# A streaming encoder layer on eight cores: the head's loads and statistics in another order

## The reference, cut to what matters

```python
h = rmsnorm(x, g_pre)
xa, ba, ca, za, xb, zb, ga, gb = split(h @ w_in)     # 8 x 1024 columns
ya = ((ba * conv3(ca * xa)) * silu(za)) @ w_a_out
d_g = mean_W(xb_g) - xb_g                            # W in (2, 4, 8, 16) by channel group
yb = (((d_g @ w_grp[g]) * pool_scale) * silu(zb)) @ w_b_out
o = (sigmoid(ga) * ya + sigmoid(gb) * yb) @ w_o
x1 = x + rmsnorm(o, g_post)
out = x1 + (p @ w_ple) * sigmoid(x1 @ w_pgate)
```

## Time and profile before

| | |
|---|---|
| median of 3 timed runs | 755.54 us (755.41 to 755.64) |
| the profiled execution | 757.77 us |
| its span, slowest core | 756.1 us (core 0) |
| other cores | 749.6 to 753.0 us |
| TensorE busy | 735.2 us, 97% of the span |
| VectorE, GpSimd, ScalarE busy | 58%, 52%, 32% |
| DMA, mean over the span | 111 GB/s |

### The profile page before, as it was taken

One profiled execution on the slowest core, in us unless ns is written; L12 is line 12 of the kernel. 1 busy time (PEld: TensorE's weight loads), 2 busy tenths in 40 slices (PEclk: granted clock), 3 DMA queues, 4 the chain that ended last, 5 costly groups with the idle time before them and its releaser, 6 DMA issues.

```text
span 756.1 us, 13493 instructions; the slowest of 8 cores (749.6 to 756.1 us)
## 1 busy us (share of the span) xinstructions
PE 735.2 (97%) x4131; PEld 367.1 (49%) x4201; DVE 441.8 (58%) x745; ACT 245.6 (32%) x454; POOL 395.6 (52%) x498
## 2 busy tenths in 40 slices
PE   6899989999999999999999999999999999999997
PEld 3774434444444444454545454545554554554443
DVE  3567455575775656346464555567767456454755
ACT  3433333323221212243333433323332222214442
POOL 3332435548876873533435262637686856731552
PEclk9999999999999999999999999999999999999999
DMA  8989877756656856885364644335333606334564
GB/s 192 215 149 181 85 166 141 132 82 112 113 89 98 130 91 127 116 137 120 72 102 125 93 95 104 76 79 85 52 67 70 112 9 104 59 116 89 156 157 141
DMA packets 67034, 83.92 MB, mean 111 GB/s; under 512 B 35858, under 2 KB 37394, under 8 KB 66964
## 3 DMA queue, kind: packets, MB, share of 16 engines
q0 software_dynamic: 31152, 48.31, 42.2%
q1 hardware_dynamic: 35664, 34.66, 18.1%
q10 hardware_dynamic: 148, 0.08, 0.1%
HBM read 115.25 MB, written 9.26 MB: 165 GB/s over the span
## 4 chain that ended last, share of the span: by engine, by line
PE 91%; DMA 5%; DVE 1%; issue 1%; POOL 1%; ACT 0%; SPq 0%; DVEq 0%; ACTq 0%; POOLq 0%
PE ps L525 57%; PE ps L710 12%; PE ps L782 8%; PE ps L817 8%; DMA slab<-w_in 3%; PE ps L539 2%; PE ps L640 2%; PE ps L811 2%; DMA xt<-xp 2%; DVE qT L613 0%; POOL tmp L609 0%; POOL slab L412 0%; DVE tmp L719 0%; PE ps L487 0%; DVE qT L647 0%
## 5 line engine op out<-in xcount | busy, mean ns | idle before, releaser
L525 PE MATMUL ps<-hT,slab 128*128 128x512 bf16 (+1 forms) x1920 | 348.0, 337 | 1.7
L525 PEld LDWEIGHTS ps<-hT,slab 128*128 128x128 bf16 x1952 | 170.5, 98 | 171.9 <-issue 2.4
L412 POOL DMA_DIRECT2D slab<-w_in x128 | 70.8, 557 | 53.0 <-PE ps L525 37.8
L609 POOL TENSOR_TENSOR tmp<-XB 128x526 f32<-128x526 f32 (+1 forms) x40 | 41.6, 1041 | 74.9 <-ACT XB L595 74.0
L609 POOL TENSOR_TENSOR tmp<-tmp 128x524 f32<-128x524 f32 (+5 forms) x60 | 63.2, 1053 | 3.2 <-POOL tmp L609 0.4
L782 PE MATMUL ps<-wo_sb,mT 128*128 128x512 bf16 x268 | 61.8, 379 | 0.2
L525 PE MATMUL ps<-vT,slab 128*128 128x512 bf16 (+1 forms) x314 | 61.4, 346 | 0.3
L525 PE MATMUL ps<-qT,slab 128*128 128x512 bf16 (+1 forms) x313 | 61.1, 346 | 0.4
L613 DVE SCALAR_TENSOR_TENSOR qT<-tmp,XB 128x512 bf16<-128x512 f32 (+1 forms) x40 | 29.8, 744 | 43.8 <-POOL tmp L609 43.5
L583 ACT ACTIVATE tmp<-U,smallT 128x512 f32<-128x512 f32 (+1 forms) x40 | 30.0, 749 | 67.8 <-DVE U L580 56.4
L828 POOL TENSOR_TENSOR xt<-xt,tmp 128x512 f32<-128x512 f32 x24 | 32.2, 1343 | 36.9 <-DVE tmp L825 35.9
(11 more groups left out here) (108 smaller groups left out, 947.9 us busy)
## 6 DMA issues: line engine op xcount, KB each, us to landing
slab<-w_in POOLq DMA_DIRECT2D x128, 256.0 KB, 6.5
xt<-xp SPq DMA_DIRECT2D x30, 512.0 KB, 7.2
yp<-xt SPq DMA_DIRECT2D x14, 512.0 KB, 3.0
slab<-w_a_out POOLq DMA_DIRECT2D x16, 256.0 KB, 6.4
slab<-w_b_out POOLq DMA_DIRECT2D x16, 256.0 KB, 5.3
wo_sb<-w_o POOLq DMA_DIRECT2D x4, 512.0 KB, 7.5
hT<-w_pgate POOLq DMA_DIRECT2D x4, 512.0 KB, 8.5
xt<-xs SPq DMA_DIRECT2D x2, 512.0 KB, 4.3
```

Of the source, the lines that this page charges most:

```text
L412: OP('pool', lambda e, d: d(e.dma_start(out=v.ap[:], in_=src)), writes=[v], sem=dsem(v, "ld"), dur=0.56, mb=0.52, key=key, nb=nb, lat=2.5 ...
L525: ins = e.matmul(b.ap[:, 0:N], lhsT=w.ap[:, kk, :], rhs=act[:, kk, k.rel:k.rel + N], start=(kk == 0), stop=(kk == nk - 1))
L609: d(e.tensor_tensor(out=twin(o.ap, k, nlo, E), in0=a, in1=b_, op=ALU.add))
```

## The change

Six edits, all but one in the first 40 us.

1. The add of tile 0's statistic is placed ahead of the second g copy on VectorE (key of that copy from -5 to 5). The planned times of the g matmuls are changed, and the second set of warm matmuls has one matmul in place of three.
2. The first slab (xa, j = 0) is loaded as fp32 by SP, second in its queue, into `U`; ScalarE casts it to its slab buffer. The other five are still loaded by GpSimd.
3. Tiles 4 to 7 are loaded into the home of `w_o` (four halves of 4 KB per partition), which is free from the start. The loads of `w_o` wait for the last use of those tiles.
4. The first part of `smallT` (for j = 0 and 1) is issued by SP in place of ScalarE, with a later key (9 for 1).
5. The planned latency after L613 is 3.0 for 1.5, in all of phase 1. No instruction is added by it; it changes only the planned order.
6. `load_res` takes ops to wait for.

```diff
@@ -309,6 +309,8 @@
         p_x = mkpool("xt", 4, [128, D], F32)
         x_late = [Buf("xtU", U[:, 0:D]), Buf("xtXB", XB[:, 0:D])]
         p_x.free += x_late
+        p_xh = Pool("xh", [Buf(f"xh{i}", wo_sb[:, 2 * i:2 * i + 2, :].rearrange("p a c -> p (a c)").bitcast(F32)) for i in range(4)])
+        xh_ops = []
         p_t = mkpool("tmp", 9, [128, TBW], F32)
         p_h = mkpool("hb", 3, [128, D], BF16)
         p_xT = mkpool("x1T", 2, [128, 8, 128], BF16)
@@ -373,8 +375,8 @@
         for h in range(2):
             OP('act', lambda e, d, h=h: d(e.dma_start(out=grow[h].ap[0:1, 0:512], in_=g_pre[0:1, h * 512:(h + 1) * 512])),
                writes=[grow[h]], sem=dsem(grow[h], "ldg"), dur=0.4, mb=0.002, key=-20 + h)
-        for j0, j1, key in ((0, 2, 1.0), (2, 8, 22.0)):
-            OP('act' if j0 == 0 else 'sp', lambda e, d, j0=j0, j1=j1: d(e.dma_start(out=smallT[:, j0:j1, :], in_=small.rearrange("p (j c) -> p j c", j=8)[:, j0:j1, :])),
+        for j0, j1, key in ((0, 2, 9.0), (2, 8, 22.0)):
+            OP('sp', lambda e, d, j0=j0, j1=j1: d(e.dma_start(out=smallT[:, j0:j1, :], in_=small.rearrange("p (j c) -> p j c", j=8)[:, j0:j1, :])),
                writes=[res(f"smallT{j}") for j in range(j0, j1)], sem=fsem(f"ld_small{j0}"), dur=0.4, mb=0.04 * (j1 - j0), key=key, nb=key)
         jb = val(p_b)
 
@@ -387,18 +389,18 @@
         gh = [val(p_b) for h in range(2)]
         for h in range(2):
             OP('pe', lambda e, d, h=h: d(e.matmul(gh[h].ap[:, :], lhsT=one.ap[0:1, 0:128], rhs=grow[h].ap[0:1, 0:512], start=True, stop=True)),
-               reads=[one, grow[h]], writes=[gh[h]], dur=1.7 - 0.6 * h, key=-8 + h)
+               reads=[one, grow[h]], writes=[gh[h]], dur=2.06, key=-8 + h)
             OP('dve', lambda e, d, h=h: d(e.tensor_copy(out=g_bc[:, h * 512:(h + 1) * 512], in_=gh[h].ap[:, :])),
-               reads=[gh[h]], writes=[res(f"g_bc{h}")], dur=0.69, key=-5)
-        OP('pe', lambda e, d: f_warm(e, d, 3), reads=[zb], writes=[jb], dur=0.7, key=-6)
+               reads=[gh[h]], writes=[res(f"g_bc{h}")], dur=0.69, key=-5 if h == 0 else 5)
+        OP('pe', lambda e, d: f_warm(e, d, 1), reads=[zb], writes=[jb], dur=0.43, key=-6)
 
         def load_gpost(key):
             OP('sp', lambda e, d: d(e.dma_start(out=g_bc[:], in_=g_post[0:1, :].partition_broadcast(128))),
                writes=[res("g_bc0"), res("g_bc1")], sem=fsem("ld_g"), dur=0.4, mb=0.5, key=key, nb=key)
 
-        def load_res(name, dst, src, k0, k1, key, extra=()):
+        def load_res(name, dst, src, k0, k1, key, extra=(), after=()):
             OP('pool', lambda e, d: d(e.dma_start(out=dst[:, k0:k1, 0:D], in_=src[k0 * 128:k1 * 128, :].rearrange("(k p) c -> p k c", p=128))),
-               writes=[res(f"{name}{k}") for k in range(k0, k1)] + list(extra), sem=fsem(f"ld_{name}{k0}"), dur=0.6 + 0.2 * (k1 - k0), mb=0.52 * (k1 - k0), key=key, nb=key)
+               writes=[res(f"{name}{k}") for k in range(k0, k1)] + list(extra), sem=fsem(f"ld_{name}{k0}"), dur=0.6 + 0.2 * (k1 - k0), mb=0.52 * (k1 - k0), key=key, nb=key, after=after)
 
         def load_wgrp(key):
             OP('pool', lambda e, d: d(e.dma_start(out=wgrp_sb[:], in_=w_grp.rearrange("(g k p) c -> p g k c", g=4, k=2, p=128))),
@@ -454,11 +456,23 @@
             return stats[:, row, gi:gi + 1]
 
 
+        slab0 = []
+
+        def first_slab():
+            v = val(p_w)
+            uu = [res("U0"), res("U1")]
+            OP('sp', lambda e, d: d(e.dma_start(out=U[:, 16:16 + D], in_=w_in[S_XA * 1024:S_XA * 1024 + 128, :])), writes=uu, sem=fsem("ld_first"), dur=0.4, mb=0.52, key=-25.5)
+            OP('act', lambda e, d: d(e.copy(out=v.ap[:].rearrange("p k c -> p (k c)"), in_=U[:, 16:16 + D])), reads=uu, writes=[v], dur=1.05, key=3.9)
+            slab0.append(v)
+
         def phase0(tl, key, by_pe):
             gi = tl.gi
-            x = val(p_x)
+            early = by_pe and gi >= 4
+            x = val(p_xh if early else p_x)
             kx = key - (30 if by_pe else 8)
             OP('sp', lambda e, d: d(e.dma_start(out=x.ap[:], in_=tl.x)), writes=[x], sem=dsem(x, "ld"), dur=0.4, mb=0.52, key=kx, nb=kx)
+            if by_pe and gi == 0:
+                first_slab()
             h = val(p_h)
             ss, rs = res(f"ss{gi}"), res(f"rs{gi}")
             OP('act', lambda e, d: d(e.activation(out=h.ap[:], in_=x.ap[:], func=AF.Square, scale=1.0 / 32.0, accum_out=stat(0, gi))),
@@ -493,6 +507,8 @@
                        reads=[b] + (first if n else []), writes=first if len(parts) > 1 and n == 0 else [ht], dur=0.69 if gi else 0.6, key=key)
                 else:
                     OP('sp', lambda e, d, hv=hv: d(e.dma_start_transpose(out=dst, in_=hv.ap[:])), reads=[hv], writes=[ht], sem=dsem(hv, "tr"), dur=1.3, mb=0.7, key=key)
+            if early:
+                xh_ops.extend(x.ops)
 
         def blkview(ap, k):
             if k.samp:
@@ -611,7 +627,7 @@
                 cur, lo, w = o, nlo, w * 2
             qr = res(f"qT{j}_{k.idx}")
             OP('dve', lambda e, d, cur=cur: d(e.scalar_tensor_tensor(out=actview(qT, j, k), in0=twin(cur.ap, k, 16, E), scalar=1.0 / W, in1=uwin(XB, k, 16, E), op0=ALU.mult, op1=ALU.subtract)),
-               reads=[cur, xr], writes=[qr], dur=d_t, key=key + 7 * dk, lat=1.5)
+               reads=[cur, xr], writes=[qr], dur=d_t, key=key + 7 * dk, lat=3.0)
             if first_prompt and sbi == 0:
                 fx = val(p_t)
                 OP('dve', lambda e, d, cur=cur: d(e.tensor_tensor(out=fx.ap[:, 0:16], in0=cur.ap[:, 16:32], in1=invcnt[:, jp, :], op=ALU.mult)),
@@ -841,7 +857,7 @@
 
         def slabs1(j, key, step):
             if j == 0 and key < 0:
-                return {s: load_slab(wblock(w_in, s * 8 + j), -20.0 + i) for i, s in enumerate(P1SECS)}
+                return {s: slab0[0] if i == 0 else load_slab(wblock(w_in, s * 8 + j), -20.0 + i, 0.5) for i, s in enumerate(P1SECS)}
             return {s: load_slab(wblock(w_in, s * 8 + j), key + step * i, 14.0 + 2.0 * i if j == 1 and key < 30 else 0.0) for i, s in enumerate(P1SECS)}
 
         def run_phase1(info, t, lead, step, stretch=1.0):
@@ -889,7 +905,7 @@
         for n, tl in enumerate(i1.tiles):
             phase0(tl, t1 + 38 + 10.0 * n, False)
         for k0 in range(0, 8, 2):
-            load_res("wo", wo_sb, w_o, k0, k0 + 2, t2 - 20 + 12 * k0)
+            load_res("wo", wo_sb, w_o, k0, k0 + 2, t2 - 20 + 12 * k0, after=xh_ops)
         t, _ = run_phase2(i0, t2, LEAD, t_homes())
         load_gpost(t - 8)
         t3 = t
```

## The result

The changed kernel takes 767.37 us in the median of four runs (766.90 to 768.41), the kernel before on the same chip 755.47 us (755.37 to 755.64): a ratio of 1.0159, 95% interval 1.0142 to 1.0177. It is 11.9 us slower where 3.8 us less was forecast. The predicted range, 749.2 to 755.2 us, does not hold it.

What follows compares the result with a forecast made beforehand. Taken as bound by TensorE on core 0, so only its idle time counts: 756.1 us span less 2.3 (head), 1.0 and 0.5 (mix waits) gives 752.3; against the 755.54 median, 751.7 us, range 749.2 to 755.2.

Steps and rivals of the forecast that it cites:

- From 27.07 to the first of these nothing waits: TensorE between the head's last slab wait at 27.07 us and the mix wait at 106.75: no waits there.
- nothing comes through: Rival 3: head's lead given back at later slabs, mix wait moves elsewhere; 755.3 us, chance 0.15.
- Head, forecast -2.3 us: Head: TensorE fed without a gap earlier; sum gave 2.8 us, bounds 0.5 and 4.0, 2.3 taken.
- The 5.2 us from landing to hT: Head: time from an x tile's landing to its finished hT, 4.5 us of work plus 0.7 of hand-overs.
- T = 25.0, n = 112: Head: TensorE fed without a gap from 25.0 us, with 112 of the 384 L539 matmuls done; gain 2.8 us.
- the 1.6 forecast: Head: with five slabs left on q0, the last lands at 25.3 us against 26.94.
- lower bound of 0.5 us for the head: Head: smallest gain, if each of tiles 4 to 7 comes 0.5 us late for its turn.
- Tiles 4 to 7 in w_o's home, forecast as free of cost: Head: wait for a free xt buffer goes, tiles land 1.9 us later; no direct cost, and 0 for w_o's loads.
- The rival's mechanism: Rival 2: late small table blocks ScalarE, tile 5's square waits behind it; 4.1 us lost, 758.6 us, chance 0.07.
- Latency, forecast -1.0: Mix matmuls (L640) planned 1.5 us later: the 0.97 us wait at 209.71 goes, 1.0 us gained.
- Below zero: up to 1.5 us once: Possible cost of the latency: later mixes hold banks and silu tiles longer, up to 1.5 us once.
- The 0.5 us for the wait near 106.75: Core 0's 2.87 us mix wait at 106.75: 0 to 1.5 us gained from the latency, 0.5 counted.

Runs made afterwards that it cites:

- xs_ahead: Changed kernel with the sample tile's load due 3 us earlier, ahead of tile 15's transposes; 763.31 us, ratio 1.0042 to the kernel before.
- x14_ahead: Changed kernel with tile 14's load ahead of tile 13's transposes again, the sample tile's kept behind tile 15's; ratio 1.0031 to the kernel before.
- swap_lat3: Kernel before with the loads of tile 14 and the sample tile due 1 us later and the latency after L613 at 3.0; ratio 1.0041.
- lat_back: Changed kernel with the planned latency after L613 at 1.5 again; 771.45 us, ratio 1.0133 to the kernel before.
- before_swap: Kernel before with the sample tile's load due 1 us later; ratio 0.9996.
- before_swap2: Kernel before with the loads of tile 14 and the sample tile due 1 us later, giving the changed kernel's order on SP; ratio 1.0001.
- b_S: Kernel before with only the first slab loaded by SP as fp32 and cast on ScalarE; ratio 1.0032.
- b_X: Kernel before with only tiles 4 to 7 in w_o's home; no ratio, spans 752.1 to 754.5 us on cores 4 to 7.
- table_early: xs_ahead with the small table's first part early on ScalarE's queue again; no ratio, spans 750.8 to 753.7 us on cores 4 to 7.
- before_lat3: Kernel before with only the planned latency after L613 at 3.0; 761.92 us, ratio 1.0024.

## Why the prediction was wrong

**The step that failed** is the one that made the sum: every edit was priced at its own place, in the head and at the mixes, and what lay between was taken to stay ("From 27.07 to the first of these nothing waits"). Order and landings there did not stay: the sum had nothing for it, and it measured some 9 of the 11.9 us (1.0159 falls to 1.0042 in xs_ahead). The runs put in its place: the sample tile's load stands behind tile 15's transposes (xs_ahead: without it no stall); its square, in ScalarE's order, stands ahead of j = 5's L599 (x14_ahead: behind it, an equally late load costs nothing); the mix follows the square by 14.10 us, not 10.88 (swap_lat3, lat_back); and SP's chain runs late. The first alone does not move the time (before_swap, before_swap2); with the old head it takes the latency as well (swap_lat3), with the new head not (lat_back). The rival "nothing comes through" named waits that move elsewhere, but priced them at nil.

**Head, forecast -2.3 us, measured +2.5.** The landings were about right: the cast ran at 8.52 (forecast 8.4 to 9.6), tile 3's square began at 19.01 (landing forecast 19.8), the small table landed at 34.5 (34). But tile 3 was ready at 28.5, not 25.0, on core 5 (26.6 to 28.2 on the others). The 5.2 us from landing to hT assumed that every engine is free for the tile. VectorE did its scaling at 24.50, behind the copy of tile 2's hT at 23.90, and that stood behind transposes which TensorE reached only after 32 matmuls at 0.112 us. The term T = 25.0, n = 112 was mis-sized: 97 were done by 27.00 on core 5, 113 in the mean. The start of the sum was, too: 27.07 is core 0's, the latest of the old heads, and their mean is 25.6 where there is such a wait. In b_S the last slab wait did end at 25.3, as forecast, but that is 0.3 us earlier and not the 1.6 forecast (26.94 to 25.3). (The lower bound of 0.5 us for the head was also a slip: 2.8 less four times 0.5 is 0.8.)

By the Trainium skill (DMA: Bandwidth & Descriptors, "Queues, rings and completion order"), a DMA engine takes its queues in turn, packet by packet. I had read from this that moving a slab to the other queue gains no transfer time. The 0.3 us of b_S agree with that better than the sum does.

The second loss of the head is the rate. Eight transposes take 0.61 us at full rate and 1.06 at half. In the kernel before they take 0.61 from 19.8 to 21.2 us on, on core 4 last; in the changed one, at 21.1 to 22.7, they still take 0.71 to 1.06 on every core. Timelines of TensorE, core 4 before and core 5 after:

```profile
21.18 0.61 PE L487 MATMUL ps<-ident_b,hb 128*128 128x128 bf16 x8
```

```profile
22.73 1.06 PE L501 MATMUL ps<-ident_b,hb 128*128 128x128 bf16 x8
```

An earlier start with the same slabs behind it spreads the work thinner. But the idle time does not explain the rate by itself. Ahead of the stretch near 18 us, TensorE's waits from 8 us on add to 4.0 to 4.8 us before, 4.7 to 6.3 in the changed kernel and only 3.3 to 4.5 in b_S, and b_S is slow too (0.091 to 0.111 us a matmul; 0.080 to 0.099 before). What keeps TensorE slow there stays open.

**Tiles 4 to 7 in w_o's home, forecast as free of cost**: alone they cost about 2 us (b_X, mark 70.8). Their loads now leave without waiting for a buffer, and a slab wait of 0.34 to 1.89 us stands near 18 to 19.5 us on every core. The loads take the slabs' place on the DMA engines: from 15 to 27 us, q0 moves 0.98 MB on core 4 of b_X and 1.22 before, q1 1.94 and 1.55 (on the other cores 0.98 to 1.02 against 1.14 to 1.21, and 1.93 to 2.03 against 1.49 to 1.59).

**Small table.** The rival's mechanism was right in kind: L599 stood at the table until 34.50 with a square behind it. It was tile 7's, not tile 5's, so it cost 0.5 to 2.7 us, not 4.1. In the mean it is 1.6 of the head's 2.5 us, and taking it away brought the mark back by 1.1 (table_early, cores 4 to 7).

**Latency, forecast -1.0.** The wait went, as forecast, and came back at 563 and 567 us (before_lat3 alone shows it). "Below zero: up to 1.5 us once" missed that the planner also puts other VectorE work ahead of the mix's producer. The 0.5 us for the wait near 106.75 has no run behind it. That wait comes and goes with the execution: before_swap and before_swap2 have none, the changed kernel has 0.99 and 1.21 us on cores 1 and 3.

**Still open.** Why SP's chain runs late. On the cores without the stall the transposes of tiles 10 and 11 go out at 79.5 to 79.8 us, against 73.8 to 75.3 on cores 4 to 7 of before_swap2, and the head's lag explains 2 to 3 us of that. On the stalled cores each lap adds more (core 0 against core 5: 99.74 and 103.70, 122.48 and 128.41), and the last load takes 9.8 us against 15.0. The laps can feed on each other, as a load waits for the transposes ahead, these for the squares, these for the loads; but why cores 1, 3, 5 and 7 and not the others was not found. Other executions stalled on other cores, as core 2 in lat_back.

## What to carry to other kernels

Where a planner orders the instructions, compare the whole order before and after an edit, on every queue, and look at the pairs that changed places far from it: here a load and a pair of transposes, 100 us behind the edited head, cost more than the head could have gained. For each load in the new order ask what stands behind its first reader on the in-order engine, and how long the chain from there to TensorE is; that chain, and not the load's lateness, sets the price. A latency given to the planner as slack can be spent on the producer itself: here the last and smallest write of the mix's input slipped behind work that waits for another engine. And a sum that starts from one core's wait should first ask how long the same wait is on the other cores.

## What was not expected of the hardware

Windows of the changed kernel, core 5: span and length, PE, PEld, DVE, ACT, POOL busy, granted clock, DMA share, GB/s.

```profile
19.36:22.93 3.57, 3.56 (x34) 3.57 (x35) 1.35 (x2) 0.80 (x2) 3.00 (x6) 1.00 1.06 225
...
162.00:163.70 1.70, 1.70 (x5) 0.58 (x6) 1.70 (x2) 0.00 (x0) 1.03 (x1) 0.50 1.12 208
```

After the wait of 9.12 us the granted clock is 0.50, that is 1.2 GHz, and the mix takes 1.87 us instead of 1.02: the stall is paid again in part. In the head, from 19.36, the matmuls run at half the rate too (0.112 against 0.061 us), but the granted clock reads 1.00; TensorE had been busy 5.01 of the 11.3 us before (8.00 to 19.30). What slows them there no run shows.

DMA queues, 90 to 150 us, core 5 after and core 1 before:

```profile
q1 hardware_dynamic: 5996, 3.93, 37.9%
```

```profile
q1 hardware_dynamic: 6012, 3.94, 29.9%
```

Nearly the same packets and bytes held the engines for more time, and the 512 KB of the sample tile took from 4.8 us (before, core 1) to 15.0 us (after, core 5) to land. Why, no run shows.
